# Encoder layer with 64 routed experts: early rows read back during the last four rounds, late rows added into a seventh row

## The reference, cut to what matters

```python
scores = sigmoid(xt @ w_router)
# 4 of 8 groups, then the best TOP_K = 6 of 64 experts of a token
w = take_along_axis(scores, idx) / sum * 2.5
hb = silu(xb @ w_e_gate[e]) * (xb @ w_e_up[e])        # 1024 -> 256
yb = (hb @ w_e_down[e]) * g                            # 256 -> 1024
routed = zeros.at[tok].add(yb)
y = routed + shared_expert(xt)
out = layer_norm(ALPHA * x + y, ln2_g, ln2_b)
```

## Time and profile before

| | |
|---|---|
| median of 3 runs | 1817.21 us (1816.81 to 1818.77) |
| profiled execution | 1814.63 us, its span 1812.5 us |
| TensorE matmul busy | 1729.1 us, 95% |
| VectorE, ScalarE, GpSimd busy | 651.7, 297.0, 150.9 us |
| DMA | 330.78 MB, mean 182 GB/s |
| mean granted clock of TensorE | 0.989 |

### The profile page before, as it was taken

How to read it: one execution, slowest core, us unless ns; L and a number is a source line. 1 busy time by engine, 2 the same in 40 slices (tenths; PEclk the granted TensorE clock), 3 DMA queues, 4 the chain that set the end, 5 groups by cost and what they waited for, 6 DMA issues and landing times.

```text
span 1812.5 us, 20130 instructions
## 1 busy us (share of the span) xinstructions
PE 1729.1 (95%) x7961; PEld 888.6 (49%) x7961; DVE 651.7 (36%) x965; ACT 297.0 (16%) x436; POOL 150.9 (8%) x147
## 2 busy tenths in 40 slices
PE   6999999999999999999999999999999999898966
PEld 3444456666666656556555544533333333333322
DVE  5011019888888874300111687400000000000018
ACT  1111112111111111112000121022222222121210
POOL 0000000000000000000000111511111111111122
PEclk9999999999999999999999999999999999999988
DMA  6114101101101001111116204799999999999857
GB/s 225 46 47 162 47 24 35 35 24 35 35 23 35 23 0 35 46 58 41 41 52 238 88 24 171 289 375 423 422 423 424 422 423 421 418 412 402 320 226 310
DMA packets 104980, 330.78 MB, mean 182 GB/s; under 512 B 8496, under 2 KB 64848, under 8 KB 86736
## 3 DMA queue, kind: packets, MB, share of 16 engines
q1 hardware_dynamic: 91520, 292.05, 40.8%
q0 software_dynamic: 13392, 37.77, 5.3%
HBM read 307.24 MB, written 33.55 MB: 188 GB/s over the span
## 4 chain that ended last, share of the span: by engine, by line
PE 79%; DVE 9%; DMA 9%; issue 1%; ACT 1%; SPq 0%; POOL 0%; DVEq 0%; POOLq 0%; ACTq 0%
PE pA L1036 14%; PE pg L669 11%; PE pg L696 10%; PE pg L819 9%; PE pB L1062 6%; PE pB L850 5%; DMA ew<-w_e_gate_up 4%; PE pB L899 2%; PE pA L899 2%; PE pA L842 2%; PE pg L709 2%; PE pB L752 2%; DMA rEF<-w_e_gate_up 2%; DMA rA<-w_e_gate_up 2%; PE pg L1023 2%; PE pA L789 1%
## 5 line engine op out<-in xcount | busy, mean ns | idle before, releaser
L696 PE MATMUL pg<-rA,hw 128*128 128x384 f32 x768 | 259.6, 486 | 0.7 <-ACT aTr L1172 0.7
L1036 PE MATMUL pA<-rCD,aTr 128*32 128x512 f32 (+2 forms) x720 | 209.2, 600 | 12.1 <-DMA rA<-w_e_gate_up 10.0
L1755 DVE TENSOR_TENSOR rows<-rows,pA 128x256 f32<-128x256 f32 x45 | 18.9, 421 | 529.8 <-ACT rows L1280 529.8
L669 PE MATMUL pg<-rEF,rA 128*128 128x512 f32 x448 | 195.0, 597 | 3.1 <-ACT rCD L1151 3.1
L696 PEld LDWEIGHTS pg<-rA,hw 128*128 128x128 f32 x768 | 140.5, 190 | 84.1 <-ACT aTr L1172 0.9
L819 PE MATMUL pg<-rA,hw 128*128 128x384 f32 x512 | 165.3, 486 | 0.0
L669 PEld LDWEIGHTS pg<-rEF,rA 128*128 128x128 f32 x448 | 85.6, 192 | 109.8 <-issue 109.8
L819 PEld LDWEIGHTS pg<-rA,hw 128*128 128x128 f32 x512 | 97.2, 190 | 67.6
L1036 PE MATMUL pA<-rA,aTr 128*32 128x512 f32 (+2 forms) x384 | 124.3, 606 | 0.0
L1036 PE MATMUL pA<-rB,aTr 128*32 128x512 f32 (+1 forms) x368 | 107.7, 599 | 4.2 <-DMA rEF<-w_e_gate_up 4.0
L1036 PE MATMUL pA<-ew,aTr 128*32 128x512 f32 (+1 forms) x352 | 107.7, 605 | 0.0
(11 more groups left out here) (318 smaller groups left out, 2344.0 us busy)
## 6 DMA issues: line engine op xcount, KB each, us to landing
rCD<-w_e_gate_up SPq DMA_DIRECT2D x21, 2048.0 KB
rA<-w_e_gate_up SPq DMA_DIRECT2D x11, 2048.0 KB
rB<-w_e_gate_up SPq DMA_DIRECT2D x11, 2048.0 KB
ew<-w_e_gate_up SPq DMA_DIRECT2D x11, 2048.0 KB, 32.7
rEF<-w_e_gate_up SPq DMA_DIRECT2D x11, 2048.0 KB
rCD<-w_e_down SPq DMA_DIRECT2D x21, 1024.0 KB
hw<-w_in SPq DMA_DIRECT2D x40, 512.0 KB, 4.1
rA<-w_e_down SPq DMA_DIRECT2D x11, 1024.0 KB
```

The lines of the kernel that those rows point to most:

```text
L669: last = mm(big_bank(fill), x1T[:, c, i * P:(i + 1) * P], strip[n % 2][:, c, :], start=(c == 0), stop=(c == KC - 1))
L696: last = mm(pg[:, n * 512:n * 512 + HALF], hw3[m][:, c, :], x1T[:, c, n * HALF:(n + 1) * HALF], start=(c == 0), stop=(c == KC - 1))
L1036: last = mm(gu[n][o:o + w, :], xT[n][:, c, o:o + w], at(gate_up_home(j % NB)[0], gate_up_home(j % NB)[1] + c * F, [[2 * D, 2], [1, F]]), s ...
```

## The change

- Rooms: rank 0 gets two units instead of one (180 in all, still 45 rounds), and the last four of the ten large experts, ranks 4 to 1, move to the end behind rank 0, each alone in a round. EARLY = 41 rounds come before them, LATE = 4.
- y_dram gets 128 spare rows. At the start POOL fills zeros, and SP zeroes rows 0 to 5 and row 7 of every token, in three portions behind strips 2, 3 and 4, and the spare rows.
- Places of the late rounds and the rest blocks get the destination token * 8 + 7 (a place without a token: the spare row of its partition), by four more small operations on VectorE; tb_ready follows them.
- scatter(t) for t >= 41, and the rest scatter, add into their rows (compute_op add), and each waits until the scatter before it has landed.
- SP reads rows 0 to 5 of tiles 0 and 1 once the scatters of the 41 early rounds have landed and their buffers are free (down of round 40, 41), then loads the rest expert, then tiles 2, 3, 4 behind rounds 42 to 44. After the last scatter: row 7 of tiles 0 and 1, rows 0 to 5 of tile 5 (whose buffer the rest expert had), row 7 of the others.
- Tiles 0 to 2: VectorE adds the six early rows into acc (those of tiles 0 and 1 behind its product of rounds 43 and 44), then the late row. Tiles 3 to 5: TensorE sums all seven rows. POOL adds nothing.
- The sum over a row comes with the last add (accum_out), ScalarE squares and sums, and results have buffers of their own (normal). The norm's gain and bias go to hw and aTr.

```diff
+LATE = 4
...
-    return [1] + [4] * 10 + [3] * 32 + [2] * 21
+    return [2] + [4] * 10 + [3] * 32 + [2] * 21
...
     large, middle, small = list(range(10, 0, -1)), list(range(11, 43)), list(range(63, 42, -1))
     first, small = small[:4], small[4:]
+    large, alone = large[:-LATE], large[-LATE:]
     mixed = sorted(((i + 0.5) / len(g), r) for g in (large, small, middle) for i, r in enumerate(g))
-    return first + [r for _, r in mixed] + [0]
+    return first + [r for _, r in mixed] + [0] + alone
...
+EARLY = NR - LATE
...
-        land = [slabs(weights[n], TOPK) for n in range(NB - 1)]
-        ln2 = weights[NB - 1][:, 0:2 * D]
+        land_at = [(E - LATE - 1 + i) % NB for i in range(NT)]
+        assert len(set(land_at)) == NT and land_at[NT - 1] == E % NB
+        land = [slabs(weights[n], TOPK) for n in land_at]
+        late = [land[i % 3][:, 1 + i // 3, :] for i in range(NT)]
+        normal = [land[i % 3][:, 3 * (i // 3), :] for i in range(NT)]
+        squares = land[0][:, 4, :]
+        ln2_g, ln2_b = hw[:, 0:D], aTr[:, 0:D]
+        zeros = hw[:, 2 * D:3 * D]
...
+                if n >= 2:
+                    for i in (2 * n - 4, 2 * n - 3):
+                        sp.wait_ge(zero_ready, 1)
+                        for first, end in ((0, TOPK), (KSTRIDE - 1, KSTRIDE)):
+                            sp.dma_start(yb[i * P:(i + 1) * P, first:end, :],
+                                         at(hw, 2 * D, [[0, end - first], [1, D]])).then_inc(y_zeroed, 16)
+            sp.dma_start(d["y_dram"][T * KSTRIDE:, :], zeros).then_inc(y_zeroed, 16)
...
+                if m == 2:
+                    sp.wait_ge(y_zeroed, ZEROED)
...
+            def load_early_rows(i):
+                sp.dma_start(land[i], yb[i * P:(i + 1) * P, 0:TOPK, :]).then_inc(s_yb[i], 16)
+
+            sp.wait_ge(y_stored[0], 16 * ((EARLY + 1) // 2))
+            sp.wait_ge(y_stored[1], 16 * (EARLY // 2))
+            for i in range(2):
+                sp.wait_ge(y_filled, EARLY + i)
+                load_early_rows(i)
+
             more = E % NB
             sp.wait_ge(resti_ready, 1)
...
+            for i in range(2, NT - 1):
+                sp.wait_ge(y_filled, EARLY + i)
+                load_early_rows(i)
+            sp.dma_start(ln2_g, d["ln2_g"].to_broadcast([P, D])).then_inc(s_ln2, 16)
+            sp.dma_start(ln2_b, d["ln2_b"].to_broadcast([P, D])).then_inc(s_ln2, 16)
+
+            def load_late_rows(i):
+                sp.wait_ge(yb_used, TOPK * (i % 3 + 1))
+                sp.dma_start(late[i], yb[i * P:(i + 1) * P, KSTRIDE - 1, :]).then_inc(s_late[i], 16)
 
             sp.wait_ge(y_stored[1 - ODD], 16 * ((NR + 1 - (1 - ODD)) // 2))
             sp.wait_ge(y_stored[ODD], rest_stores)
             sp.wait_ge(xg_loaded[1 - ODD], 16 * ((NR + 1) // 2))
             sp.wait_ge(xg_loaded[ODD], rest_gathers)
-            yb = d["y_dram"].rearrange("(t k) n -> t k n", k=KSTRIDE)
-            for i in range(NT):
-                if i == NB - 1:
-                    sp.wait_ge(sum_filled, 1)
-                    sp.wait_ge(half_added, 1)
-                    sp.wait_ge(yb_used, 1)
-                n = i % (NB - 1)
-                for m in range(2):
-                    three = slice(3 * m, 3 * m + 3)
-                    sp.dma_start(land[n][:, three, :], yb[i * P:(i + 1) * P, three, :]).then_inc(s_yb[n][m], 16)
+            load_late_rows(0)
+            load_late_rows(1)
+            load_early_rows(NT - 1)
+            for i in range(2, NT):
+                load_late_rows(i)
             for i in range(NT):
                 sp.wait_ge(out_ready, i + 1)
                 dst = d["y_prompt"][i * P:(i + 1) * P, :] if i < NTP else \
                     d["y_sample"][(i - NTP) * P:(i - NTP + 1) * P, :]
-                sp.dma_start(dst, acc[:, i, :]).then_inc(out_stored, 16)
+                sp.dma_start(dst, normal[i]).then_inc(out_stored, 16)
             sp.wait_ge(out_stored, 16 * NT)
 
 
...
+            def early_rows_summed(i):
+                pe.wait_ge(s_yb[i], 16)
+                for k in range(TOPK):
                     for m in range(2):
-                        last = mm(pairY[i % 2][:, m * 512:(m + 1) * 512], ident,
-                                  land[n][:, k, m * 512:(m + 1) * 512], start=(k == 0), stop=(k == TOPK - 3))
+                        mm(sums[i][:, m * 512:(m + 1) * 512], ident, land[i][:, k, m * 512:(m + 1) * 512],
+                           start=(k == 0), stop=False)
+
+            def late_rows_added(i):
+                pe.wait_ge(s_late[i], 16)
+                for m in range(2):
+                    last = mm(sums[i][:, m * 512:(m + 1) * 512], ident, late[i][:, m * 512:(m + 1) * 512],
+                              start=False, stop=True)
                 last.then_inc(sum_filled, 1)
+
+            pe.wait_ge(y_ready, nrest + NR)
+            early_rows_summed(3)
+            early_rows_summed(4)
+            late_rows_added(3)
+            early_rows_summed(5)
+            late_rows_added(4)
+            late_rows_added(5)
...
+                sc.wait_ge(mean_ready, i + 1)
+                fn(squares, acc[:, i, :], ACT.Square, bias=mv[:, 2 * i + 1:2 * i + 2],
+                   accum_out=std[:, i:i + 1]).then_inc(var_ready, 1)
                 sc.wait_ge(var_ready, 2 * NT + 3 + i)
-                fn(std[:, i:i + 1], std[:, i:i + 1], ACT.Sqrt).then_inc(std_ready, 1)
+                fn(std[:, i:i + 1], std[:, i:i + 1], ACT.Sqrt, scale=1.0 / D, bias=bst[:, 0:1]).then_inc(std_ready, 1)
...
+            ve.wait_ge(tok_ready, 1)
+            link(v.tensor_scalar(tbldi[:, EARLY:NCOL], tbldi[:, EARLY:NCOL], KSTRIDE - 1, None, ALU.bitwise_or))
+            link(v.tensor_copy(tbld[:, EARLY:NCOL], tbldi[:, EARLY:NCOL]))
+            link(v.tensor_scalar(tbld[:, EARLY:NCOL], tbld[:, EARLY:NCOL], float(-T * KSTRIDE), con[:, K_IOTAP:K_IOTAP + 1],
+                                 ALU.add, ALU.min))
+            v.tensor_scalar(tbldi[:, EARLY:NCOL], tbld[:, EARLY:NCOL], float(T * KSTRIDE), None, ALU.add).then_inc(tb_ready, 1)
...
+            def early_rows_added(i):
+                ve.wait_ge(s_yb[i], 16)
+                for k in range(TOPK):
+                    v.tensor_tensor(acc[:, i, :], acc[:, i, :], land[i][:, k, :], ALU.add).then_inc(yb_used, 1)
+                    ve.wait_ge(yb_used, TOPK * i + k + 1)
...
                 hidden(t)
+                if t >= NR - 2:
+                    early_rows_added(t - NR + 2)
...
             def summed(i):
-                ve.wait_ge(half_added, i + 1)
-                v.tensor_tensor(acc[:, i, :], acc[:, i, :], land[i % (NB - 1)][:, TOPK - 2, :], ALU.add).then_inc(yb_used, 1)
-                ve.wait_ge(yb_used, i + 1)
-                ve.wait_ge(sum_filled, i + 1)
-                v.tensor_tensor(acc[:, i, :], acc[:, i, :], pairY[i % 2][:, :], ALU.add).then_inc(sum_taken, 1)
+                if i < 3:
+                    ve.wait_ge(s_late[i], 16)
+                else:
+                    ve.wait_ge(sum_filled, i - 2)
+                v.scalar_tensor_tensor(out=acc[:, i, :], in0=acc[:, i, :], scalar=1.0,
+                                       in1=late[i] if i < 3 else sums[i][:, :],
+                                       op0=ALU.mult, op1=ALU.add, accum_out=mv[:, 2 * i:2 * i + 1]).then_inc(sum_taken, 1)
                 ve.wait_ge(sum_taken, i + 1)
-                statistics(acc[:, i, :], i, D)
-                v.tensor_scalar(std[:, i:i + 1], mv[:, 2 * i + 1:2 * i + 2], LN_EPS, None, ALU.add).then_inc(var_ready, 1)
+                link(v.tensor_scalar(mv[:, 2 * i + 1:2 * i + 2], mv[:, 2 * i:2 * i + 1], -1.0 / D, None, ALU.mult))
+                v.tensor_scalar(mv[:, 2 * i:2 * i + 1], mv[:, 2 * i:2 * i + 1], 1.0 / D, None, ALU.mult).then_inc(mean_ready, 1)
+                ve.wait_ge(mean_ready, i + 1)
                 if i == 0:
                     ve.wait_ge(s_ln2, 32)
-                centred(acc[:, i, :], i, ln2[:, 0:D])
+                link(v.scalar_tensor_tensor(out=normal[i], in0=acc[:, i, :], scalar=mv[:, 2 * i:2 * i + 1], in1=ln2_g,
+                                            op0=ALU.subtract, op1=ALU.mult))
 
...
+                v.scalar_tensor_tensor(out=normal[i], in0=normal[i], scalar=rstd[:, i:i + 1], in1=ln2_b,
+                                       op0=ALU.mult, op1=ALU.add).then_inc(out_ready, 1)
+
+            early_rows_added(2)
             summed(0)
...
+            g.memset(zeros, 0.0).then_inc(zero_ready, 1)
...
+                if t == 0:
+                    po.wait_ge(y_zeroed, ZEROED)
+                if t < EARLY:
+                    g.indirect_dma_start(d["y_dram"], bass.IndirectOffsetOnAxis(tbldi[:, t:t + 1], 0), yrow[t % 2], None,
+                                         bounds_check=T * KSTRIDE - 1, oob_is_err=False).then_inc(y_stored[t % 2], 16)
+                else:
+                    po.wait_ge(y_stored[(t - 1) % 2], 16 * ((t - 1) // 2 + 1))
```

(38 more changed lines are left out.)

16 lines of the change are left out of this document (1 added, 15 removed).

## The result

The changed kernel is slower by half a percent: 1826.18 us (median of 4 runs, 1825.34 to 1827.53) against 1817.99 for the kernel before, measured beside it; ratio 1.0049, 95% interval 1.0034 to 1.0063. (The ratios in this document are estimates over all runs and differ from the quotient of the medians by up to 0.0005, or 0.9 us.) The forecast was 1811.5, with "faster" the likeliest side; the time lies in the range, on the side of the slow adds. The profiled execution took 1825.79 us, its span is 1823.9 (1812.5 before).

What follows compares the result with a forecast made beforehand. TensorE and DMA are both full in the rounds, then DMA idles before the returning rows. Tables and order +11, later last landing +6.9, tail -23.6 give -5.7 on the 1817.2 median: 1811.5 us, range 1801 to 1830.

Steps and rivals of the forecast that it cites:

- the slow adds: Case in which late adding scatters are slow and the kernel ends near 1825.7 us; chance 0.31.
- Zeroing, tables: Zero stores at the start cost nothing; four small chained operations ahead of tb_ready cost 1.0 us.
- Order (+10): Large experts moved to the end make round 40 start later: 9.9 us, bounds 4 and 12.
- up(39): Sign in the rounds: the prediction is wrong if this step doesn't stall.
- Early reads (0, bound 5): Reads and adds of early tiles during the last rounds stay hidden: 0 us, bound 5.
- The adding scatters (11.5 each, 6 for the last): Five chained late scatters at the rounds' end: four of 11.5 us, one of 6, last landing at 1764.8.
- X: Landing of the last scatter, after the rounds; forecast at 1764.8 us.
- the 1757: Sign on the rest block's scatter: the prediction is wrong if it issues much after 1757 us.
- The tail (X + 42): Work after the last scatter's landing ends 42 us later, against 65.6 before: -23.6 us.
- the chain of adds decides: Rival: POOL's waits between late scatters set the end; 18.3 us each under load, X = 1779, 1825.7 us; chance 0.31.
- The half-rate rule: Skill's rule that reducing transfers run at about half a copy's rate; loaded adds would come near 18 us.

Runs made afterwards that it cites:

- experiment 4: The kernel before with only the new rooms and order of experts: 1822.86 us, ratio 1.0027.
- experiment 1: The changed kernel with the five late scatters as plain writes instead of adds, all waits kept: 1820.89 us, ratio 1.0022.
- experiment 2: The changed kernel with each early read of a tile issued as six DMAs of one row (4 KB) per token: 1818.51 us, ratio 1.0008.
- experiment 9: The changed kernel without the gather behind the rest block, its turn on TensorE and the copy to xT: 1825.46 us, ratio 1.0041.
- experiment 5: The changed kernel with late scatters plain, each into its own table, no waits between them, late additions left out: 1818.10 us, ratio 1.0006.

## Why the prediction was wrong

The sum for the span was 1806.8; it is 1823.9, 17.1 more. (The medians are 14.7 apart, 1826.18 against 1811.5: the sum started from an execution 2.6 faster than its median, the changed kernel's profile is 0.4 below its own.) By its steps:

- **Zeroing, tables: right.** Round 0's product comes at 1182.53, 0.86 later than in the kernel before (1181.67); I took 1.0. The stores cost nothing.
- **Order (+10): too high.** Round 41 is 8.7 later, 0.9 of it the tables; alone the order cost 7.4 at that round and about 5 in the time (experiment 4). Its working had a wrong step as well, and up(39) was named as a sign: the stall was to come ahead of round 39, but it stands ahead of round 38, with 15.62 us idle, and round 39 follows at the usual distance (11.85). That the size came out near is partly luck. So the chain of late scatters began at 1710.36, not 1712.8: 2.4 in favour.
- **Early reads (0, bound 5): outside the chain.** Tile 0 came 3 us later than I had it (1725.1 against 1722), its adds held the product of round 44 by 4 us, and the rest weights came 2 us late (TensorE waited till 1739.80). Both are real, and both vanish behind POOL's chain, as its rows show: the scatters wait for one another.
- **The adding scatters (11.5 each, 6 for the last): the step that failed.** They took 15.0, 12.3, 14.8, 14.4 and 6.3 us: 62.8 instead of 52. Taking "near the plain scatter under load" was the error: the 10.7 of the earlier trace rows was read beside loads of weights, whose pieces are 16 and 8 KB per partition, and the new load consists of pieces of 24 KB. The plain scatter itself takes 11.0 to 13.5 there (experiment 1), and with pieces of 4 KB the add is down at 9.1 to 11.0 (experiment 2). The add as such was worth 1.4. A part may also be that a late scatter writes all 128 rows, where the 10.7 skipped places without a token: on emptier queues that is 4.9 against 3.3 us plain. Under load no run separates it.
- **Links of the chain: left out.** Between a landing and the next issue lie 0.8 us three times, and 3.4 before the rest scatter, which the changed program puts behind the held gather: 5.9 us in which I had counted 0. So X came at 1779.1 instead of 1764.8: 10.8 and 5.9 more, 2.4 less. The rest scatter went out at 1772.75, much after the 1757 that the prediction gave as the sign of being wrong.
- **The tail (X + 42): nearly right.** It was 44.8. VectorE takes 4.4 per tile as said. TensorE was 3 us later than worked out, and by either way: in the change behind the turn of the held gather, without it (experiment 9) behind the late row at the lower clock. I had looked at what the new wait delays for ScalarE and TensorE's rounds and missed the gather queued behind it on POOL.

The rival "the chain of adds decides" named place and time (X = 1779, 1825.7 us) and came true, but not by its price: it had 18.3 us for each loaded add, and 14.1 plus the links made up the same sum. The half-rate rule of the Trainium skill ("Collectives: The Full Stack", "The bandwidth ceiling: the fold count and why AG ≠ RS ≠ AR") didn't hold for these small transfers: an add took 14.1 us against 12.8 for a plain scatter in its place (means of the four under load), and 6.3 against 4.9 on emptier queues, 1.1 and 1.3 times as long. That rule is about rates, and no run here measures the rate of adding transfers by themselves.

Where the gain went, by the times: order alone is +4.9 (0.27% of 1817), the tail alone -5.6 (0.31%), the whole change +8.9 (0.49%). If these add up, which wasn't tested, the overlap with all that serves it costs 9.6 (by the medians 5.8, -5.1 and +8.2, which leaves 7.5, so the split is good to some 2 us). Of that, 7.8 hang on waits and additions together (the change against experiment 5, 1.0049 against 1.0006); some 2 remain, no more than that uncertainty; rows read under load and 26 MB more to move would be candidates. What stays open is how a DMA engine divides its time between the two kinds of queue; the runs show only that the way the reads are cut moves a scatter's latency.

## What to carry to other kernels

Filling idle DMA time pays only if nothing on the path to the end shares the queues: price every small transfer there under the new load, with the pieces in which the new load comes, and count the links between them. A wait put before a series makes a chain; list what stands behind it on the same engine, even what seems to have no reader. Time the parts of a bundle alone: here the plainest one, the tail's passes, was the only gain (ratio 0.9969).

## What the runs showed of the hardware

- Scatters of rows of 4 KB took 3.3 us on empty queues (places without a token skipped) and 4.9 with all 128 rows written, 10.7 beside loads in pieces of 16 and 8 KB per partition (places skipped), 11.0 to 14.4 beside reads of 24 KB per partition (experiments 1 and 5), all 128 rows written, and 17.7 when issued 5 us behind another.
- An addition added 1.4 us to that, in the mean of four under load and on emptier queues alike. Beside reads in pieces of 4 KB a scatter with its addition took 9.1 to 11.0 (experiment 2).
- The gather of the rest block, 2.2 us on empty queues, took 11.0 and 21.9 us beside the reads of 24 KB.
- At the same DMA share, from 1720 to 1760, reads in pieces of 4 KB beside adding scatters moved 374 and 356 GB/s, whole ones 391 to 397; whole ones beside plain scatters 424 and 428.
- A scatter that waits for the one before goes out 0.8 us after that one's landing.
- After 9.7 us of waiting TensorE came back at a granted clock of 0.50, and four matmuls took 3.78 us instead of 1.88 (experiment 9).
